# Rotated key columns in two passes, with the high and low parts of their weights side by side in one stationary tile

## The reference

```python
def odd_layer(x, cos, sin, norm_g, w_in, ...):
    h = rms_norm(x, norm_g)
    c_q, c_kv, k_rope, z = jnp.split(
        h @ w_in, [Q_LORA, Q_LORA + KV_LORA, Q_LORA + KV_LORA + QK_ROPE], axis=-1)
    ...
    k = jnp.concatenate(
        [k_nope, jnp.broadcast_to(k_rope[:, :, None, :], (B, S, MLA_HEADS, QK_ROPE))], axis=-1)
    q = rope_tail(rms_norm(q, q_head_g), cos, sin)
    k = rope_tail(rms_norm(k, k_head_g), cos, sin)
```

## Time and profile before

| | |
|---|---|
| median of 3 runs | 999.0 us (997.13 to 1000.02) |
| profiled execution, device time | 1001.95 us |
| its span, first to last instruction | 1000.2 us |
| mean granted TensorE clock | 0.991 |
| TensorE matmul busy | 989.7 us (99%), 5931 records |
| VectorE, ScalarE, GpSimd busy | 694.4, 517.2, 278.1 us |

### The profile page before, as it was taken

One profiled execution on the slowest core, in us unless ns is written; L12 is line 12 of the kernel. 1 busy time (PEld: TensorE's weight loads), 2 busy tenths in 40 slices (PEclk: granted clock), 3 DMA queues, 4 the chain that ended last, 5 costly groups with the idle time before them and its releaser, 6 DMA issues.

```text
span 1000.2 us, 15813 instructions
## 1 busy us (share of the span) xinstructions
PE 989.7 (99%) x5931; PEld 772.1 (77%) x5931; DVE 694.4 (69%) x1241; ACT 517.2 (52%) x970; POOL 278.1 (28%) x354
## 2 busy tenths in 40 slices
PE   9999999999999999999999999999999999999998
PEld 8788444444788888888888999997777888777887
DVE  5698899999844533312443699998999999996311
ACT  7344544335332322222243667866999999997000
POOL 0002242240000001100001377876764325551000
PEclk9899999999999999999999999999999999999999
DMA  9220431111154433121112063576587565530322
GB/s 294 36 64 22 106 85 43 43 43 43 64 168 135 139 127 109 44 63 44 31 33 79 22 226 130 203 198 192 127 185 180 128 129 123 107 106 2 113 87 73
DMA packets 166380, 103.65 MB, mean 104 GB/s; under 512 B 76320, under 2 KB 150560, under 8 KB 166048
## 3 DMA queue, kind: packets, MB, share of 16 engines
q1 hardware_dynamic: 159216, 102.25, 36.8%
q10 hardware_dynamic: 7088, 0.39, 0.5%
HBM read 56.48 MB, written 29.36 MB: 86 GB/s over the span
## 4 chain that ended last, share of the span: by engine, by line
PE 80%; DVE 11%; ACT 3%; issue 2%; DMA 2%; POOL 1%; SPq 0%; DVEq 0%; ACTq 0%; POOLq 0%
PE banks L106 23%; PE banks L108 22%; PE banks L107 22%; PE banks L2077 6%; PE banks L2095 3%; PE banks L2096 1%; DVE front_set_b L893 1%; DMA front_w<-in_w_in_ab 1%; DVE front_t_form L869 1%; DMA heads_kv_raw<-in_w_ukv 1%; DVE front_w_row L876 1%; DVE heads_probs_big L1884 1%; DVE front_sums L776 1%; PE banks L2104 1%; DVE heads_y L1875 1%
## 5 line engine op out<-in xcount | busy, mean ns | idle before, releaser
L106 PE MATMUL banks<-front_act_hi,front_w_hi 128*128 128x512 f32 x368 | 146.7, 399 | 0.0
L108 PE MATMUL banks<-front_act_hi,front_w_lo 128*128 128x512 f32 x368 | 145.0, 394 | 0.0
L107 PE MATMUL banks<-front_act_lo,front_w_hi 128*128 128x512 f32 x368 | 144.9, 394 | 0.0
L1892 DVE TENSOR_TENSOR heads_pt_lo<-banks,heads_pt_hi 128x512 f16<-128x512 f32 (+2 forms) x192 | 102.0, 553 | 11.1 <-ACT heads_pt_hi L1764 6.6
L1764 ACT ACTIVATE heads_pt_hi<-banks 128x512 f16<-128x512 f32 (+2 forms) x192 | 88.6, 484 | 5.7 <-PE banks L2077 5.5
L106 PEld LDWEIGHTS banks<-front_act_hi,front_w_hi 128*128 128x128 f32 x368 | 70.3, 191 | 15.2 <-issue 0.5
L107 PEld LDWEIGHTS banks<-front_act_lo,front_w_hi 128*128 128x128 f32 x368 | 70.3, 191 | 14.9 <-issue 0.5
L108 PEld LDWEIGHTS banks<-front_act_hi,front_w_lo 128*128 128x128 f32 x368 | 70.1, 190 | 14.9
L2095 PE MATMUL banks<-heads_v,heads_pt_hi 128*128 128x128 f16 x576 | 74.8, 220 | 0.0
L2077 PE MATMUL banks<-ident,heads_probs_big 128*128 128x128 f32 x416 | 69.5, 281 | 1.0 <-ACT heads_probs_big L1755 1.0
L526 POOL TENSOR_TENSOR front_sq<-front_sq,front_squares 128x1024 f32<-128x1024 f32 x6 | 14.4, 2398 | 199.1 <-ACT front_squares L720 199.1
(11 more groups left out here) (352 smaller groups left out, 2639.4 us busy)
## 6 DMA issues: line engine op xcount, KB each, us to landing
qk_scratch<-heads_y SPq DMA_DIRECT2D x22, 512.0 KB, 3.8
front_w<-in_w_in_c SPq DMA_DIRECT2D x17, 512.0 KB, 4.0
front_x<-in_x_t SPq DMA_DIRECT2D x16, 512.0 KB, 5.3
front_raw<-in_w_in_ab SPq DMA_DIRECT2D x14, 512.0 KB, 5.1
qk_scratch<-heads_last_y SPq DMA_DIRECT2D x10, 512.0 KB, 3.7
front_w<-in_w_out_ab SPq DMA_DIRECT2D x8, 512.0 KB, 3.7
x_scratch<-front_x SPq DMA_DIRECT2D x8, 512.0 KB, 4.0
v_scratch<-heads_v SPq DMA_DIRECT2D x32, 128.0 KB, 3.1
```

The lines of the kernel that those rows point to most:

```text
L106: nc.tensor.matmul(out, w_hi, a_hi, start=first, stop=False, skip_group_check=resumed)
L107: nc.tensor.matmul(out, w_hi, a_lo, start=False, stop=False, skip_group_check=resumed)
L108: return nc.tensor.matmul(out, w_lo, a_hi, start=False, stop=last, skip_group_check=resumed)
L1892: nc.vector.tensor_tensor(pt_lo[:, q % PIECES, :width], t_ps[:, banks[("piece", n, k)] % 3, :width], pt_hi[:, q % PIECES, :width], ALU.sub ...
```

## The change

The 32 low weight columns of the rotary tile are written beside the 32 high ones, into columns 32 to 63 of the same stationary tile. Two matmuls then do for each row block and half: that tile with the high activations, and that tile with the low ones. Rows 0 to 31 of the result hold the products of the high weights, rows 32 to 63 those of the low weights. ScalarE copies 64 rows. At the turning, each transpose becomes two float32 matmuls that accumulate in PSUM, one with columns 0 to 31 and one with columns 32 to 63 of a 64-row slice of the identity as the moving operand, which adds the two halves. The added term low by low was left out before.

```diff
--- before.py
+++ after.py
@@ -727,7 +727,7 @@
                     nc.scalar.activation(trig[:], red[:], ACT.Sin).then_inc(trig_done, 1)
             elif n == ROPE0:
                 act.wait_ge(proj_ready, n + 1)
-                nc.scalar.activation(krt[0:ROPE, :], proj[0:ROPE, ring_bank(n)], ACT.Copy).then_inc(lat_out, 1)
+                nc.scalar.activation(krt[0:2 * ROPE, :], proj[0:2 * ROPE, ring_bank(n)], ACT.Copy).then_inc(lat_out, 1)
             else:
                 i = n - Z0
                 act.wait_ge(evacuated, LAT0 + i + 1)
@@ -760,7 +760,11 @@
 
         def low(n):
             dve.wait_ge(hi_done, n - RING + len(STEPS) + 1)
-            nc.vector.tensor_tensor(weight(n, 2), weight(n, 0), f32(weight(n, 1)), ALU.subtract).then_inc(lo_done, 1)
+            if n == ROPE0:
+                nc.vector.tensor_tensor(weight(n, 1)[:, :, ROPE:2 * ROPE], weight(n, 0)[:, :, :ROPE],
+                                        f32(weight(n, 1))[:, :, :ROPE], ALU.subtract).then_inc(lo_done, 1)
+            else:
+                nc.vector.tensor_tensor(weight(n, 2), weight(n, 0), f32(weight(n, 1)), ALU.subtract).then_inc(lo_done, 1)
 
         def x_low(k, done, cols=slice(0, S)):
             dve.wait_ge(x_high, done)
@@ -1163,6 +1167,10 @@
         def product(n, k, c, first, last):
             cols = slice(c * BANK, (c + 1) * BANK)
             hi, lo = operands(n)
+            if n == ROPE0:
+                out, both_parts = proj[:, ring_bank(n), cols], weight(n, 1)[:, k]
+                nc.tensor.matmul(out, both_parts, hi[:, k, cols], start=first, stop=False)
+                return nc.tensor.matmul(out, both_parts, lo[:, k, cols], start=False, stop=last)
             return three_passes(nc, proj[:, ring_bank(n), cols], weight(n, 1)[:, k], weight(n, 2)[:, k],
                                 hi[:, k, cols], lo[:, k, cols], first, last)
 
@@ -1323,8 +1331,10 @@
                                          start=True, stop=True)
                 pe.wait_ge(lat_out, LAT + 1)
                 for t in range(NT):
-                    last = nc.tensor.transpose(turned_ps[:, t], krt[0:ROPE, t * P:(t + 1) * P],
-                                               ident[0:ROPE, 0:ROPE])
+                    for part in range(2):
+                        last = nc.tensor.matmul(turned_ps[:, t], krt[0:2 * ROPE, t * P:(t + 1) * P],
+                                                ident[0:2 * ROPE, part * ROPE:(part + 1) * ROPE],
+                                                start=part == 0, stop=part == 1)
                 last.then_inc(small_ready, 1)
     return sync, scalar, vector, gpsimd, tensor
```

## The result

| | before | after |
|---|---|---|
| median of 20 runs | 998.85 us (996.99 to 1000.02) | 1000.04 us (998.25 to 1001.96) |
| profiled execution, device time | 1001.95 us | 1001.54 us |
| its span | 1000.2 us | 999.7 us |
| mean granted clock | 0.991 | 0.990 |

The ratio is 1.0016, 95% interval 1.0011 to 1.0022: slower by 1.1 to 2.2 us (the two medians lie 1.2 us apart), and within the 0.3% that I had set as no change. The two profiled executions lie at different places of their distributions: the one of before 3 us above its median and above all of its 20 timed runs, the one of after 1.5 us above its median. So I compare them by stage and leave the spans alone. The ratios of fast runs leave out three of the twelve executions of the later run e3, which took 1666.69, 2576.33 and 2576.26 us; no trace of them was kept and their cause is open.

What follows compares the result with a forecast made beforehand. TensorE was taken to bound the kernel, busy 989.7 of 1000.2 us. Tile -3.63, transposes removed -0.99, new records +6.83, rest 0 gave +2.2 us on a 999.0 us median: 1001.2 us, range 997.8 to 1003.2 us.

Steps and rivals of the forecast that it cites:

- terms 1 and 5: Rotary tile: 48 matmuls become 32, -3.63 us, all on the path; copies, weight preparation and waits elsewhere: nothing.
- the slack: Weights for a later tile are ready early: more than 10 us remain though the shorter tile asks 3.63 us sooner.
- term 3, first part: Turning: 16 float32 calls leave 32 records, 0.112 us apart at full clock or 0.213 at half.
- term 3, second part: Turning: all 32 new records run at half clock, +6.83 us.
- late-clock rival: Clock falls only after the turning's new records, which cost 3.6 us: -1.7 us in all, 997.3 us; chance 0.11.
- term 4: Dense matmuls behind the turning: half clock already loses 2.0 us there; no difference taken, +0.5 us as near end.
- slower rival: Low clock lasts longer on dense matmuls behind the turning: +3.4 us, 1002.4 us; chance 0.27.
- cheap-call: Turning's new calls leave one record each at the transposes' step, 2.0 us: -2.6 us in all, 996.4 us; chance 0.05.
- lost-gain: Shorter tile's gain does not arrive, a later tile waiting for weights: +3.6 us more, 1004.8 us; chance 0.02.

Runs made afterwards that it cites:

- e3: Changed kernel with one float32 matmul call per token block instead of two, using a stacked identity; 0.9987 of the kernel before (0.9972 to 1.0003).
- e1: Changed kernel with the old turning of eight transposes, so the two-pass tile alone; 0.9962 of the kernel before, 3.8 us faster.
- e2: Kernel before with the new turning alone, the second call of each pair multiplying with zeros; 1.0061 of the kernel before, 6.1 us slower.
- e10: The changed kernel run once more, nothing altered; 1.0019 of the kernel before (1.0009 to 1.0028), stage 50.5 us.
- e6: Changed kernel with the one-column calls spread through the tile before the turning, the turning left in one piece; 1.0000 of the kernel before.
- e9: Changed kernel with one-column calls and turning calls both spread among the dense matmuls of one tile; 0.9991 of the kernel before, 0.9 us faster.
- e7: Kernel before with each one-column call placed ahead of three dense matmuls, nothing else; 0.9971 of the kernel before, 2.9 us faster.
- e8: Changed kernel with eight 64-row transposes, halves added on VectorE, and one-column calls spread; 0.9939 of the kernel before, 991.75 us.
- e4: Changed kernel with eight 64-row transposes instead of the turning's matmuls, VectorE adding the halves; 0.9960 of the kernel before, 993.73 us.

## Why the prediction was right, step by step

The direction of the sum, its class (no change by 0.3%) and its mechanism held: forecast +2.2 us, measured +1.6 us (1.1 to 2.2), 1000.04 us in a range of 997.8 to 1003.2. That the forecast came within 0.6 us owes something to luck, because its largest term moves by over 1 us from one execution to the next (below).

*The tile* (terms 1 and 5): -3.63 us forecast, 3.63 us read in the trace, 3.8 us measured alone in e1. No gap in front of a later tile, as the slack had said.

*Thirty-two records and their step* (term 3, first part): 32 records, 0.116 and 0.213 us apart where 0.112 and 0.213 were forecast. Bounding the 32-column matmul by rows with 1 and with 128 columns was enough, and so was counting the records of line 1322 instead of its calls. One reading was less sure than it was written: that line 1280 ran its 128-column matmuls at half clock was inferred from their step. The window of before over them says 1.00 (length, busy us and records of PE and PEld of line 1280, clock, DMA):

```profile
1.05:6.83 5.78, 5.78 (x27) 5.78 (x28) 1.00 0.80 225
```

In favour of the inference, the last five records of this line start 0.11 us apart, so 128 columns have both steps. For 32 columns the rows above now show both steps with the clock beside them. The chain of the earlier trace rows is also 80% TensorE, not three quarters, which changes nothing in the sum.

An estimate by calls would have halved the cost; e3 shows the size of that error, 2.9 us.

*The clock under them* (term 3, second part) is the mis-sized step. I took all 32 records at half clock, 6.83 us, because the fall had come 2.70 us after the small matmuls began. In the two profiles of the changed kernel it came after 4.29 and 5.51 us, and the turning took 6.31 and 5.22 us; in e2 and e3, after 3.1 us, all were at half clock (6.96 us for 32 in e2). One profile gives one place of the fall and no fixed distance. The sum also gave the one-column records no gain, and they took 3.55 and 3.56 us in the two profiles instead of 4.28 us, because the later fall left them at full clock. With these, the stage adds up: in the profile of after -3.63 (tile) - 0.73 (one-column) + 5.32 (turning) + 0.2 (dense part) = +1.2 us, and in e10 -3.63 - 0.72 + 4.23 - 0.3 = -0.4 us, against +1.1 and -0.5 us read from the timelines. How the +1.6 us of the ratio is spread over executions is not shown beyond these two; the timed halves e1 and e2 carry it. The late-clock rival was the right kind of doubt with the right sign; as written, with all 32 at full clock, it happened in no profile with the turning behind the one-column matmuls in a row.

*The dense matmuls at half clock* (term 4): 4.67 and 3.56 us in the changed kernel, 4.26 us in the kernel before. No difference, to within what one profile tells. The slower rival needed over 6.0 us; 5.93 us in e3 is the longest seen, and 5.78 us in e2 the next, so that rival was nearer than the changed kernel's own profiles tell.

*The Trainium skill's estimate.* By the Trainium skill's page TensorE: Matmul & The Clock Gate, section LDWEIGHTS (loading the stationary operand), an estimate for 32 records is 3.4 us. At full clock e6 has them in 469.44 - 465.76 = 3.68 us, near that; at half clock they took nearly twice as much, 6.96 us in e2. The Trainium skill's 25 ns for a small matmul (the same page, section Back-to-back issue gap) does appear as a distance of starts, but not as a price: of the two one-column records shown in e9, 0.28 us in all, the second is 0.25 us long, so they start 0.03 us apart, yet such a pair cost 0.24 us in e7. In a row no plain float32 records with 128 stationary columns start less than 0.11 us apart. Transposes do: (0.71 - 0.22) / 7 = 0.07 us apart at full clock in e8, which moves 64 columns from a 64-row tile.

The cheap-call and lost-gain rivals are refuted by e2 and e1.

## What to carry to other kernels

Count the records that a call leaves, and price a small float32 matmul by its weight load: here two loads for each plain call, in a row at the same step for 64 or 128 rows and for 1 or 32 moving columns, and one short load for a transpose. Before small matmuls are added to a stretch that is already thin, look at the granted clock there: at half clock each costs double. Placing them between dense matmuls gave 2.9 us here (e7), and adding on an engine that idles about 5.6 us against the changed kernel (e4), next to the 3.6 us of the passes saved. When a gain and a cost nearly cancel and the clock falls nearby, one profile cannot size the rest; give that term both clock prices.

## What the runs showed of the hardware that I had not expected

The granted clock fell at a different place of the same program in its two profiled executions: 4.29 and 5.51 us after the same instruction, 1.6 us apart in the stage. From that instruction to each fall TensorE was busy without a gap, with one-column and 32-column matmuls alone. Even the kernel before had been paying: 2.9 us came back when its one-column matmuls were spread (e7). And small matmuls between dense ones are not always as cheap as in a row: 0.12 us each with a 128-row tile alone (e7), but 0.165 us when 64-row ones stand beside them (e9), where the next weight load began only after the last had ended.
